# The right half of the last four token tiles made on POOL instead of VectorE, at the end of a two-block transformer kernel

## The reference

```python
h = rms_norm_2(x, pre_ffn_norm[l])
f = (jax.nn.silu(h @ w_gate[l]) * (h @ w_up[l])) @ w_down[l]
x = x + rms_norm_2(f, post_ffn_norm[l])
```

## Time and profile before

| | |
|---|---|
| runs (us) | 2172.86, 2172.51, 2170.12; median 2172.51 |
| the profiled execution's own time | 2170.35 us |
| its span, first to last instruction | 2168.6 us |
| mean granted TensorE clock | 0.979 |
| PE busy | 2035.3 us, 94% of the span |
| DVE busy | 1227.5 us, 57% |
| POOL busy | 831.5 us, 38% |

### The profile page before, as it was taken

One profiled execution on the slowest core, in us unless ns is written; L12 is line 12 of the kernel. 1 busy time (PEld: TensorE's weight loads), 2 busy tenths in 40 slices (PEclk: granted clock), 3 DMA queues, 4 the chain that ended last, 5 costly groups with the idle time before them and its releaser, 6 DMA issues.

```text
span 2168.6 us, 26861 instructions
## 1 busy us (share of the span) xinstructions
PE 2035.3 (94%) x10069; PEld 1691.6 (78%) x10069; DVE 1227.5 (57%) x1551; ACT 776.6 (36%) x1195; POOL 831.5 (38%) x438
## 2 busy tenths in 40 slices
PE   2999999999999999979999899894999999999997
PEld 2788888888887778857888689783788888887885
DVE  5776666656545346565140444227765655565977
ACT  4344444434420112141200676226333333224453
POOL 2333333232333435523454000144655555534552
PEclk9999999999999999989999999997999999999998
DMA  9111101111111101242111000042233333347344
GB/s 358 56 40 30 39 29 39 29 35 33 41 51 47 39 30 49 77 162 64 49 48 48 20 1 1 22 144 78 83 102 116 102 99 98 103 136 271 98 136 150
DMA packets 152208, 170.79 MB, mean 79 GB/s; under 512 B 8822, under 2 KB 105543, under 8 KB 151112
## 3 DMA queue, kind: packets, MB, share of 16 engines
q1 hardware_dynamic: 145432, 153.46, 22.0%
q10 hardware_dynamic: 6704, 16.36, 2.0%
HBM read 137.03 MB, written 32.77 MB: 78 GB/s over the span
## 4 chain that ended last, share of the span: by engine, by line
PE 87%; DVE 6%; ACT 3%; issue 2%; DMA 1%; ACTq 0%; SPq 0%; POOL 0%; DVEq 0%
PE psum L626 8%; PE psum L628 8%; PE psum L627 8%; PE psum L646 7%; PE psum L648 7%; PE psum L647 7%; PE psum L1089 6%; PE psum L1090 6%; PE psum L1091 6%; PE psum L758 3%; PE psum L1046 3%; PE psum L1155 3%; PE psum L1157 3%; PE psum L1156 3%; PE psum L1035 2%
## 5 line engine op out<-in xcount | busy, mean ns | idle before, releaser
L555 POOL TENSOR_TENSOR w_hi<-w_raw,ones 128x1024 fp32r<-128x1024 f32 x92 | 223.6, 2431 | 965.8 <-PE psum L648 467.7
L626 PE MATMUL psum<-h_hi,w_hi 128*128 128x512 f32 x768 | 311.4, 405 | 1.6 <-POOL w_lo L558 1.1
L628 PE MATMUL psum<-h_hi,w_lo 128*128 128x512 f32 x768 | 301.0, 392 | 0.0
L627 PE MATMUL psum<-h_lo,w_hi 128*128 128x512 f32 x768 | 300.3, 391 | 0.0
L646 PE MATMUL psum<-w_hi,h_hi 128*128 128x512 f32 x704 | 276.1, 392 | 11.3 <-DVE h_lo L1974 4.3
L647 PE MATMUL psum<-w_lo,h_hi 128*128 128x512 f32 x704 | 275.3, 391 | 0.0
L648 PE MATMUL psum<-w_hi,h_lo 128*128 128x512 f32 x704 | 275.3, 391 | 0.0
L558 POOL TENSOR_TENSOR w_lo<-w_raw,w_hi 128x1024 fp32r<-128x1024 f32 x92 | 254.2, 2763 | 7.2
L1187 ACT ACTIVATE arena<-psum 128x1024 f32<-128x1024 f32 (+7 forms) x127 | 95.8, 761 | 251.3 <-PE psum L628 164.0
L626 PEld LDWEIGHTS psum<-h_hi,w_hi 128*128 128x128 f32 x768 | 145.3, 189 | 33.5 <-issue 4.2
L628 PEld LDWEIGHTS psum<-h_hi,w_lo 128*128 128x128 f32 x768 | 144.8, 189 | 31.2
(11 more groups left out here) (300 smaller groups left out, 4081.5 us busy)
## 6 DMA issues: line engine op xcount, KB each, us to landing
w_raw<-w_in SPq DMA_DIRECT2D x68, 512.0 KB, 3.7
act_op<-arena SPq DMA_DIRECT2D x77, 256.0 KB, 2.2
arena<-act_op SPq DMA_DIRECT2D x77, 256.0 KB, 2.7
w_raw<-w_out SPq DMA_DIRECT2D x24, 512.0 KB, 3.5
w_raw<-w_gate SPq DMA_DIRECT2D x22, 512.0 KB, 4.0
w_raw<-w_up SPq DMA_DIRECT2D x22, 512.0 KB, 5.1
arena<-ada_w SPq DMA_DIRECT2D x8, 1024.0 KB, 14.2
x_mid<-arena ACTq DMA_DIRECT2D x16, 512.0 KB, 2.7
```

The lines of the kernel that those rows point to most:

```text
L555: pool.tensor_tensor(w_hi[:, c, :].rearrange("p (a n) -> p a n", n=P), raw.rearrange("p (a n) -> p a n", n=P), unit_scale, ALU.mult).then_ ...
L626: pe.matmul(o, wh, xh, start=(k == 0), stop=False)
L627: pe.matmul(o, wh, xl, start=False, stop=False)
L628: return pe.matmul(o, wl, xh, start=False, stop=(k == KT - 1))
```

## The change

For the last four token tiles the row product, the scaling by `rstd` and the addition of the residual of the right half go to POOL, as three instructions per tile (DVE had two, since one of its instructions multiplies and adds). DVE keeps the sum from PSUM, the mean square, the reciprocal and the left half. SP waits for both halves. Two semaphores that are no longer in use by then count POOL's steps.

```diff
@@ program
+        y2_step, Y2_0, x2_done, X2_0 = s0_done, 4, w_rounded, U_DOWN
@@ SyncE, sending the tiles
             for a, t in enumerate(range(NT)):
                 sp.wait_ge(res_done, 2 * NT + a + 1)
+                if a >= 4:
+                    sp.wait_ge(x2_done, X2_0 + a - 3)
                 sp.dma_start(ap["out"][t], (XB, XA)[t // 4][:, t % 4, :]).then_inc(out_sent, 16)
@@ GpSimd, after its last split
+            for t in range(4):
+                y2, x2 = w_raw[:, t, 0:HALF], XA[:, t, HALF:]
+                pool.wait_ge(sums_out, OUT0 + D_OUT["C12"] + t + 1)
+                TT(y2, c12[:, t, :], ROW_F[:, HALF:D], ALU.mult).then_inc(y2_step, 1)
+                pool.wait_ge(y2_step, 2 * t + 1 + Y2_0)
+                pool.wait_ge(rstd_done, M_RES[2] + 4 + t + 1)
+                pool.tensor_scalar(y2, y2, rstd[:, 4 + t:5 + t], None, ALU.mult).then_inc(y2_step, 1)
+                pool.wait_ge(y2_step, 2 * t + 2 + Y2_0)
+                TT(x2, x2, y2, ALU.add).then_inc(x2_done, 1)
@@ VectorE, token_out
-                for half in range(2):
+                for half in range(2 if i < 4 else 1):
                     w = STT(...)
@@ VectorE, the last four tiles
                 out_sum(NPR - 1, t)
-                y2 = w_raw[:, t, 0:HALF]
-                dve.wait_ge(sums_out, OUT0 + D_OUT["C12"] + t + 1)
-                TT(y2, c12[:, t, :], ROW_F[:, HALF:D], ALU.mult).then_inc(ycp_done, 1)
                 token_ms(4 + t, 4 + t, 12 + t, 13 + t)
-                token_out(4 + t, 4 + t, XA[:, t, :], (c11[:, t, :], y2), 32 + 12 + t + 1)
+                token_out(4 + t, 4 + t, XA[:, t, :], (c11[:, t, :],), 32 + 12)
```

## The result

| | before | changed |
|---|---|---|
| median of nine runs (us) | 2171.0 | 2176.53 |
| lowest and highest | 2168.26, 2172.86 | 2173.08, 2178.59 |
| ratio | | 1.0027, 95% interval 1.0017 to 1.0036 |
| profiled execution, its own time and span | 2170.35, 2168.6 | 2178.59, 2176.8 |

The change makes the kernel slower by 5.5 us.

The account below looks back on a forecast made before the run. A DVE chain bounds the end, then POOL: reload 7 us plus four scalings of 2.0 less 1.8 gives +13.2 us; added to the profiled 2170.35 or median 2172.51, 2183.5 or 2185.7, stated as 2185, range 2178 to 2192.

Parts of the forecast that it names:

- What bounds the end, and what DVE gains: Last four tiles: a DVE chain including ACT's square and root; dropping the right half saves 0.66 us per tile, 2.64 in all.
- Slower, and POOL the bound: Last four tiles: POOL's three instructions take 4.70 us per further tile against DVE's 2.78, so the end comes 13.2 us later.
- The forecast's own sign of being wrong: Prediction is wrong if POOL's first scaling starts within 2 us of the product's end; two other signs were also named.
- The reload ends at 2160.33: Library reload behind POOL's first product, taken as 7 us from 2153.33; the first scaling cannot start before its end.
- rival 2: Reload passed over or nearly free, scaling 1.0 to 2.4 us: 4.8 to 10.4 us slower; chance 0.12.
- the two formulas: Added time at the end: r + 4s - 1.8 with a reload of r us, 0.8 + 4s without; s is the scaling.
- The scaling at 2.0 us: POOL's tensor_scalar by rstd in each of the last four tiles: 2.0 us taken, range 1.3 to 2.4.
- The line-rate rule: One-input POOL operations run roughly at line-rate: scaling 0.43 us plus start, sum 6 us less; a short-scaling rival, chance 0.14.
- The collisions without a reload, 0.6 us in each later tile: With a free reload, DVE's left half (0.5) and mean square (0.1) push between POOL's instructions in each further tile.
- the case with a reload: The forecast's main case: POOL delayed by 7 us, colliding only with DVE's last mean square and left half, 0.5 us in all.
- DVE's tiles: DVE at the end: four periods of 2.8 us, only the last mean square and left half stretched.
- The range: Measured time 2178 to 2192 us, from +6 to +20 about a start of 2172; some 0.17 chance left out.

Follow-up runs that it names:

- run 5: Changed kernel with the right half of the last four tiles made by neither engine: those tiles took 11.17 us (13.82 before the change), time ratio 0.9986.
- Run 4: Changed kernel without DVE's left half of the last four tiles: from their first sum to the last addition 18.31 us (changed kernel 19.36).
- runs 1 and 2: Changed kernel with three more resident-library reloads before each scaling: last four tiles 20.01 us; with another library's instruction before the first scaling: 11.4 us longer than changed.
- run 10: Changed kernel with 96 tiny two-input DVE instructions behind the last left half, as probes while POOL finishes: last four tiles 19.38 us.
- run 8: Changed kernel with the mean square as a tensor_scalar, one tensor and a scalar column: last four tiles 19.17 us (changed kernel 19.36).
- run 3: Changed kernel with the scaling as a tensor_tensor whose second operand is rstd repeated over the columns: last four tiles 17.59 us (changed kernel 19.36).
- runs 6 and 7: Kernel before with only the row product on POOL: last four tiles 15.51 us; the same with mean square as tensor_scalar with scalar column: 14.10 us.

## Why the prediction was wrong

- **What bounds the end, and what DVE gains: right.** A chain on DVE before, POOL after; 2.65 us of gain for DVE (run 5) against 2.64.
- **Slower, and POOL the bound: right.** Product and addition at 1.26 to 1.29 us, waits of 0.08 to 0.09 between them. Run 4 shows that POOL sets the period. The forecast's own sign of being wrong came true all the same: the first scaling starts 0.64 us behind the product, within its 2 us.
- **"The reload ends at 2160.33": wrong, and the main step.** It was costed as a load, on the ground that the build had put it there. It costs as much only where another library is in place: 0.08 us against 5.8 and 7.0 (runs 1 and 2). The forecast named this case as rival 2 and gave it 0.12. Nothing in the trace of the kernel before spoke for the forecast against it; both ends of the bound, nothing and 37 us, were open, and the value taken was a choice of the price of a load without asking whether there was one. By the two formulas this is 7 - 1.8 - 0.8 = 4.4 us too much.
- **The scaling at 2.0 us: mis-sized.** It takes 1.56 undisturbed. Four times 0.44 is 1.8 us too much. The value lies in the range given and nearer to the row of its own size, 1.29, than the one taken. The line-rate rule of the Trainium skill (GPSIMD Engine Reference, Engine selection), by the forecast's estimate 0.43 us and something for the start, is not borne out: with one tensor input the instruction is slower than one with two.
- **The collisions without a reload, 0.6 us in each later tile: mis-sized.** With s = 1.56 the formula 0.8 + 4s gives 7.0, and 5.54 was measured. The first tile agrees (5.29 us to the next product against 5.48), and so does the second (4.82 against 4.86). The third and the fourth have 4.22 and 4.26, where 4.86 was assumed: 1.2 us of the 1.5. Two things were missed. DVE's tiles are shorter than POOL's, so that its last left half comes in POOL's third tile and the fourth is free of it; this was seen in the case with a reload and forgotten in the case without. And a tensor_scalar holds DVE up for less than half of its time (run 10), so that the third left half passed through (0.75 us at 2163.37, with POOL's scaling from 2162.20 to 2163.76).

4.4 + 1.8 + 1.5 = 7.7 is the whole way from +13.2 to +5.5.

- **DVE's tiles: wrong.** Four periods of 2.8 us were forecast, with only the last mean square and left half stretched. The sums start 3.22, 3.35 and 3.14 us apart, since POOL, without a load to wait for, works beside DVE from the first tile on. It cost nothing at the end, where POOL is last.
- **The range** left out the lower part of rival 2, and the result is there. Its low end took in a short scaling or a free reload, but not a free reload with fewer collisions: by the forecast's own formula rival 2 with the measured scaling is 0.8 + 4 x 1.56 = 7.0 us, inside the range, and the collisions that did not come, 1.5 us, take the result out of it.

## What to carry to other kernels

Moving work to an idle engine pays only if that engine can keep the period of the one it relieves: here 2.78 us per tile were left on VectorE, and POOL's pace without any collision is 4.2 (run 4), so the change was lost before any contention. Where a build adds an instruction by itself, find out first whether it does anything in this state, and only then what it costs; the two cases go into the forecast as equals when no row tells them apart. Where POOL has to work beside VectorE, short two-input VectorE instructions on a chain of waits are worth rewriting to one tensor and a column of scalars, but on a chain with many meeting points a stall removed in one place can come back in another (run 8).

## What the runs showed of the hardware that was not expected

- A POOL tensor_scalar of 128 x 512 with a column of scalars takes 1.56 us, a tensor_tensor of the same size 1.26 to 1.29, and a tensor_tensor whose second operand is that column repeated takes 1.37 us right behind a collision (run 3).
- The tensor_scalar holds up VectorE's two-input instructions only for about the first half microsecond of its 1.56, a tensor_tensor for nearly all of its 1.26 us (run 10). The Trainium skill (SBUF — State Buffer, Who interferes with whom) has the loser blocked for the whole instruction. The tensor_tensor rows agree with that, the tensor_scalar rows don't, and the measurement decides. Why the hold ends so early was not tried.
- A VectorE tensor_scalar of 128 x 1 whose second operand is a column of scalars in SBUF runs through a POOL product at 0.22 us, where the form with two tensors takes 0.60 (runs 6 and 7).
- A reload of POOL's library that is in place costs 0.08 us, a switch 5.8 or 7.0 (runs 1 and 2).
